# Expert weights with two consecutive rows per partition, and the operands that follow them read with a step of two

## What is computed

```python
N_EXPERTS = 16; EXPERT_FF = 1024; CAPACITY_FACTOR = 2
def expert_choice_ffn(h, router_w, w_gate, w_up, w_down):
    cap = CAPACITY_FACTOR * n // N_EXPERTS          # 64 tokens for each expert
    aff = jax.nn.softmax((h @ router_w).astype(jnp.float32), axis=-1)
    w_sel, idx = lax.top_k(aff.transpose(0, 2, 1), cap)
    xs = jax.vmap(lambda hb, ib: hb[ib])(h, idx)
    hid = jax.nn.silu(jnp.einsum('becd,edf->becf', xs, w_gate)) * jnp.einsum('becd,edf->becf', xs, w_up)
    ys = jnp.einsum('becf,efd->becd', hid, w_down) * w_sel[..., None].astype(h.dtype)
    return jax.vmap(lambda yb, ib: jnp.zeros((n, d), h.dtype).at[ib.reshape(-1)].add(yb.reshape(-1, d)))(ys, idx)
```

## Time and profile before

| | us |
|---|---|
| time of a run: median of 3 (lowest, highest) | 2821.27 (2818.16, 2821.94) |
| span of the profiled execution, first to last instruction | 2814.1 |
| what lies around the span, against the median | 7.2 |
| TensorE busy in the span | 2697.8 |
| expert stage on PE: first and last start of line 1952 | 1377.2 and 1850.9 |

### The profile page before, as it was taken

One profiled execution on the slowest core, in us unless ns is written; L12 is line 12 of the kernel. 1 busy time (PEld: TensorE's weight loads), 2 busy tenths in 40 slices (PEclk: granted clock), 3 DMA queues, 4 the chain that ended last, 5 costly groups with the idle time before them and its releaser, 6 DMA issues.

```text
span 2814.1 us, 32083 instructions
## 1 busy us (share of the span) xinstructions
PE 2697.8 (96%) x12682; PEld 1796.7 (64%) x12682; DVE 1246.7 (44%) x2310; ACT 523.0 (19%) x870; POOL 171.2 (6%) x140
## 2 busy tenths in 40 slices
PE   7999999999899999999799999989999999999997
PEld 3688888887544444586344333334496877888886
DVE  4255656664444344535311111146573335654644
ACT  3122121222233233211100000022322113100001
POOL 1122211220000000132000000000000000000000
PEclk9999999999999999999899999999999999999999
DMA  9622111211111111225599999942102421233330
GB/s 346 212 60 57 54 52 45 60 30 38 38 53 53 45 53 49 79 75 183 231 409 409 409 409 409 409 154 64 42 1 83 125 77 46 78 87 90 90 90 30
DMA packets 327673, 374.57 MB, mean 133 GB/s; under 512 B 10033, under 2 KB 273030, under 8 KB 324230
## 3 DMA queue, kind: packets, MB, share of 16 engines
q1 hardware_dynamic: 327286, 371.93, 38.6%
q10 hardware_dynamic: 272, 1.05, 0.1%
HBM read 370.85 MB, written 2.10 MB: 133 GB/s over the span
## 4 chain that ended last, share of the span: by engine, by line
PE 91%; DVE 4%; DVEq 1%; DMA 1%; ACT 1%; issue 1%; SPq 0%; ACTq 0%
PE psum L1650 31%; PE psum L1952 12%; PE psum L1381 8%; PE psum L2108 6%; PE psum L720 3%; PE psum L1118 2%; PE psum L1837 2%; PE psum L815 2%; PE psum L728 2%; PE psum L2642 2%; PE psum L1878 2%; PE psum L705 2%; PE psum L1308 2%; PE psum L1360 2%; PE psum L1337 1%; PE psum L2724 1%
## 5 line engine op out<-in xcount | busy, mean ns | idle before, releaser
L1650 PE MATMUL psum<-arena 128*128 128x256 f32 x4144 | 907.9, 378 | 1.0 <-ACT arena L2740 0.5
L1650 PEld LDWEIGHTS psum<-arena 128*128 128x128 f32 x4144 | 779.2, 189 | 116.2 <-issue 5.3
L1952 PE MATMUL psum<-arena 128*64 128x512 f32 x1536 | 347.6, 597 | 3.0 <-issue 2.1
L1952 PEld LDWEIGHTS psum<-arena 128*64 128x64 f32 x1536 | 104.9, 136 | 217.5 <-issue 214.4
L1381 PE MATMUL psum<-arena 128*128 128x512 f32 x512 | 233.1, 597 | 0.0
L2108 PE MATMUL psum<-arena 128*128 128x512 f32 (+1 forms) x448 | 168.1, 532 | 0.0
L1682 DVE TENSOR_TENSOR arena<-psum,arena 128x256 f32<-128x256 f32 x66 | 28.0, 425 | 315.2 <-ACT arena L1695 192.6
L1381 PEld LDWEIGHTS psum<-arena 128*128 128x128 f32 x512 | 92.4, 189 | 104.1 <-issue 104.1
L1883 DVE SCALAR_TENSOR_TENSOR arena<-psum,arena 128x512 f32<-128x512 f32 x64 | 48.0, 750 | 246.4 <-PE psum L1878 245.8
L2108 PEld LDWEIGHTS psum<-arena 128*128 128x128 f32 x448 | 84.8, 190 | 80.8 <-issue 77.3
L1657 POOL TENSOR_TENSOR arena<-arena 128x512 f32<-128x512 f32 x34 | 48.2, 1418 | 1119.7 <-DMA arena<-in_w_in 653.3
(11 more groups left out here) (378 smaller groups left out, 3202.9 us busy)
## 6 DMA issues: line engine op xcount, KB each, us to landing
arena<-in_w_gate SPq DMA_DIRECT2D x64, 1024.0 KB, 18.3
arena<-in_w_up SPq DMA_DIRECT2D x64, 1024.0 KB, 16.2
arena<-in_w_down SPq DMA_DIRECT2D x64, 1024.0 KB, 18.0
arena<-in_w_in SPq DMA_DIRECT2D x120, 512.0 KB, 4.0
arena<-in_ada_w SPq DMA_DIRECT2D x24, 1024.0 KB, 7.4
arena<-in_w_up SPq DMA_DIRECT2D x32, 512.0 KB, 5.3
arena<-in_w_down SPq DMA_DIRECT2D x32, 512.0 KB, 4.8
arena<-in_w_out SPq DMA_DIRECT2D x16, 512.0 KB, 3.8
```

Of the source, the lines that this page charges most:

```text
L1650: mm = pe.matmul(psum[:, base + b, c * HALF:(c + 1) * HALF], w, v, start=(first and q == 0 and m in (0, 2, 3, 4)), stop=(last and q == KC ...
L1952: mm = pe.matmul(psum[64 * e:64 * e + 64, bank + n, :], tokens(e, 2 * q + k), w[:, k, 512 * n:512 * n + 512], start=(q == 0 and k == 0), s ...
```

## The change

The view of the expert weights is changed, so that partition p of quarter q now holds the rows 256q + 2p and 256q + 2p + 1. These two follow each other in HBM: one run of 8 KB for each partition, where there were two of 4 KB. The same 256 rows come with a unit as before, and each DMA still moves 1 MB to the same slot.

Block k of a quarter now carries every second row. The operands that must match it are therefore formed from every second column: the gather's stationary operand `h2tok`, and the transposes' stationary operand `e_hid`, are read with a step of two elements (8 bytes), 128 elements out of a stretch of 256, starting at 0 or at 1. So `xs` and `e_hidT` come out with the matching rows, and what reads them is unchanged.

```diff
@@ pe_gather
-                    mm = pe.matmul(psum[:, 6 + half, k * P:(k + 1) * P], h2tok[:, t, (4 * half + k) * P:(4 * half + k + 1) * P],
+                    mm = pe.matmul(psum[:, 6 + half, k * P:(k + 1) * P], pair_rows(h2tok[:, t, :], 4 * half + k),
                                    hot[i % 2][:, t, :], start=(t == 0), stop=(t == LT - 1))
@@ the views
-        w_ff = [A[n][0].rearrange("e (q k p) n -> e q p k n", p=P, k=2) for n in ("w_gate", "w_up", "w_down")]
+        w_ff = [A[n][0].rearrange("e (q p k) n -> e q p k n", p=P, k=2) for n in ("w_gate", "w_up", "w_down")]
+
+        def pair_rows(ap, c):
+
+            return ap[:, 2 * P * (c // 2):2 * P * (c // 2) + 2 * P].rearrange("p (m k) -> p k m", k=2)[:, c % 2, :]
@@ pe_experts
                         mm = pe.transpose(psum[:, half, c * P:(c + 1) * P],
-                                          e_hid[:, (4 * half + c) * P:(4 * half + c + 1) * P], ident)
+                                          pair_rows(e_hid, 4 * half + c), ident)
```

## The result

| | us |
|---|---|
| before: median of 13 runs (lowest, highest) | 2821.88 (2817.76, 2827.09) |
| changed: median of 13 runs (lowest, highest) | 2827.74 (2822.48, 2829.05) |
| ratio changed / before, 95% interval | 1.0018, 1.0009 to 1.0026 |
| span of the changed kernel's profiled execution | 2825.9 |

By the ratio the changed kernel is slower by 0.18%, 5.1 us; the medians lie 5.9 us apart (a ratio given here is not the quotient of the two medians beside it). The interval leaves no change out and reaches from 2.5 to 7.3 us. The forecast was "no change".

A forecast was written before the change was run, and what follows sets the result against it. The prediction took TensorE (PE) to bound the kernel, with DMA just keeping pace. Transfers 0 and reads 0 left the span at 2814.1 us; with 7.2 us around it, 2821.3, forecast as 2821 us, range 2812 to 2842.

The forecast's parts named there:

- PE sets the pace, DMA just keeps it: Expert stage: both are full, but PE waits for no DMA; a pair of experts takes 61.30 us.
- Transfers, 0: Expert weight loads: 8 KB runs save 17 us of DMA time, hidden behind PE, so worth 0.
- Matmuls not disturbed by the DMA traffic: Expert matmuls: lighter DMA traffic could gain at most 4.8 us; taken as 0.
- Reads with a step: Stationary loads of gather and hidden transposes: a step of two costs 0 to 65.3 us; taken as 0.
- The upper bound: The same stepped loads lasting twice as long: 58.4 us for the gather plus 6.9 for the turns, 65.3 us.
- Rival 1: Stepped loads on PE are slower: 2828 us if a tenth longer, 2886.6 if doubled; chance 0.15.
- the likeliest case: Whole kernel: no change, 2821 us, with its own range of 2816 to 2827; chance 0.72.
- Rival 2: Last expert weight units: 8 KB runs stream slower than 4 KB runs, 2840 us at 391 GB/s; chance 0.05.
- Rival 3: A small gain from matmul time or idle time tied to DMA traffic, at most 6.9 us, 2814 us; chance 0.08.
- 7.2 us around the span: Whole kernel: time around the profiled span of 2814.1 us against the median, added to reach 2821.3 us.

The follow-up runs named there:

- The runs alone: 8 KB weight runs kept, gather and hidden turns reading whole columns again, against the kernel before: 2820.64 us against 2822.19, ratio 0.9998.

## Why the prediction was wrong

- *"PE sets the pace, DMA just keeps it"*: right. The runs alone moved 421 GB/s in place of 409, and the pair kept 61.30 us.
- *Transfers, 0*: right. The forecast rate was 424 GB/s; the landing times fell as said. The DMA share, though, is still 1.00 in the late pair, where I had it below full; only the rate fell, to 407.
- *Matmuls not disturbed by the DMA traffic*: right, a pair is as long at 421 as at 409 GB/s.
- *Reads with a step: "Between the ends I take 0"*: **this step failed.** The choice rested on counting elements ("as many to fetch"). The number of elements does not set the price: a load with a step of two is 8 ns longer, 0.120 for 0.112 us, for as many elements. Two half gathers and a turn make 0.67 us of a pair, 0.62 on the chain. The term that was put at 0 measured 4.4 us in the stage and, with an estimated 0.5 for the first gather, 4.9 in all; the step alone, without 8 KB runs, brought the whole loss. The bounds held (0 to 65.3 us), but the cost lies near the lower end and not at it, and the gather had no cover, as the text said: the load's 7% came out at the matmul.
- *The upper bound*: a load that lasts twice as long is what a step of four gives, 233 ns. The share of it for the turns, 6.9 us, was wrong in kind: turns take at most 0.14 us more, 13%, at any step tried.
- *Rival 1* was what happened, at its small end. It priced a tenth more at 6.5 us, 2828 us; by its sum 7% would be 4.6 us, and the profile has 4.9. That the measured 2827.74 us fits its 2828 so closely is luck: the medians are 5.9 us apart, and the interval is 4.8 us wide. It had 0.15, mostly for the upper end. The range 2812 to 2842 us holds the time; the likeliest case's own 2816 to 2827 doesn't, by 0.7 us. Nor is 0.2% what it takes to tell a change from none: the interval reaches only 0.09% to either side.
- *Rival 2* fell: 8 KB runs stream faster. The 391 GB/s of the start were those of the small loads beside them, or of something else; the runs here don't show which. *Rival 3* fell with them.
- *"7.2 us around the span"*: the runs that have both numbers show 1.7 to 3.5 us around it, mostly 1.8 (2827.74 and 2825.9, say). So the profiled execution of before was a short one, and the rest of the 7.2 was the scatter of executions. The forecast didn't hang on it.

## What to carry to other kernels

Where TensorE's loads and matmuls run nose to tail, as in this float32 gather with 128 columns against 128, a step in either operand is on the path: 7% for two elements in the stationary one, 4% in the moving one, and about double at four. Transposes paid 6 to 13% at any step. Put a reordering where it is free: here in what ACT and DVE read, with adjacent writes. And before buying transfer speed, look whether the engine that uses the data ever waits for it; a DMA share of 1.03 is no wait.

## What the runs showed that I had not expected

- The distance between the gather's stationary loads fits the count of 16-byte lines that it touches, 1.82 to 1.87 ns each: 120, 175, 233 and 238 ns at steps of 2, 3, 4 and 8 (float32, 128 columns), with a floor of 112. The transposes' loads don't follow it.
- DVE's product of 128 x 1024 takes 1.22 us with operands read at a step of two, and 1.93 us when it writes elements alternately to two blocks 512 bytes apart; ACT's copy of 128 x 512 goes from 0.60 to 1.09 us by such a write.
- Transposes take 1.22, 1.20, 1.23 and 1.16 us for eight at steps of 2, 3, 4 and 8, against 1.09 without: a small price that doesn't grow, though the stepped data is their stationary operand too.
- 1 MB loads stream at 421 GB/s in runs of 8 KB and at 409 in runs of 4 KB.
